# The seams between stages of a two-layer encoder: which squares the running sum takes, the fill products before a broadcast, and the order of products in the query, key, value stage

## The reference, cut to what matters

```python
for layer in range(2):
    h = h + 0.5 * rms_norm(swiglu(rms_norm(h, g[0]), w_in[layer, 0], w_out[layer, 0]), g[1])
    hn = rms_norm(h, g[2])
    m = attention_mixer(hn, ...) if layer % 2 == 0 else recurrent_mixer(hn, ...)
    h = h + rms_norm(m, g[3])
    h = h + 0.5 * rms_norm(swiglu(rms_norm(h, g[4]), w_in[layer, 1], w_out[layer, 1]), g[5])
return h[:, 16:]
```

## Time and profile before

| | |
|---|---|
| Median of 3 runs | 1137.19 us (1136.44, 1137.19, 1138.9) |
| Profiled execution, span from the first to the last instruction | 1134.5 us, 21273 instructions |
| PE / PEld / DVE / ACT / POOL busy | 96 / 92 / 63 / 49 / 10 % of the span |
| Mean granted TensorE clock | 0.991 of full |
| DMA | 169.65 MB, mean 150 GB/s |

### The profile page before, as it was taken

One profiled execution on the slowest core, in us unless ns is written; L12 is line 12 of the kernel. 1 busy time (PEld: TensorE's weight loads), 2 busy tenths in 40 slices (PEclk: granted clock), 3 DMA queues, 4 the chain that ended last, 5 costly groups with the idle time before them and its releaser, 6 DMA issues.

```text
span 1134.5 us, 21273 instructions
## 1 busy us (share of the span) xinstructions
PE 1094.0 (96%) x8622; PEld 1048.0 (92%) x8622; DVE 717.5 (63%) x1036; ACT 556.7 (49%) x830; POOL 114.5 (10%) x103
## 2 busy tenths in 40 slices
PE   6999999999999999999999999999997699999998
PEld 5999999998547999999999999999997699999997
DVE  5766655575554666665467666544889967666542
ACT  4544454453556554444445454444596556454541
POOL 3000000043000200000010000000377401000000
PEclk9999999999999999999999999999998899999999
DMA  8654445715002254635653644457153163645541
GB/s 250 212 190 148 162 149 184 247 61 174 1 1 73 77 186 158 203 111 182 198 187 127 201 155 148 150 184 243 55 186 111 38 223 112 211 160 176 170 137 38
DMA packets 166464, 169.65 MB, mean 150 GB/s; under 512 B 3312, under 2 KB 165416, under 8 KB 166392
## 3 DMA queue, kind: packets, MB, share of 16 engines
q1 hardware_dynamic: 166088, 168.16, 45.5%
q0 software_dynamic: 96, 0.28, 0.1%
q10 hardware_dynamic: 208, 0.20, 0.1%
HBM read 167.30 MB, written 1.05 MB: 148 GB/s over the span
## 4 chain that ended last, share of the span: by engine, by line
PE 88%; DVE 8%; ACT 1%; issue 1%; DMA 1%; POOL 0%; SPq 0%; DVEq 0%; ACTq 0%
PE bank L358 25%; PE bank L360 25%; PE bank L359 25%; PE bank L607 2%; PE bank L579 2%; DVE h L1120 1%; PE bank L593 1%; PE bank L386 1%; DVE mg L1116 1%; DVE xl L1083 1%; PE bank L366 1%; DVE gm L1368 1%; PE bank L479 1%; PE bank L377 1%; PE bank L374 1%
## 5 line engine op out<-in xcount | busy, mean ns | idle before, releaser
L1077 DVE TENSOR_TENSOR wl<-raw,wh 128x2048 fp32r<-128x2048 f32 (+2 forms) x178 | 366.3, 2078 | 173.8 <-ACT wh L717 173.4
L358 PE MATMUL bank<-xh,wl 128*128 128x272 f32 (+1 forms) x1552 | 448.5, 289 | 9.3 <-DVE xl L1373 7.8
L360 PE MATMUL bank<-xh,wh 128*128 128x272 f32 (+1 forms) x1552 | 446.6, 288 | 0.0
L359 PE MATMUL bank<-xl,wh 128*128 128x272 f32 (+1 forms) x1552 | 445.1, 287 | 0.0
L717 ACT ACTIVATE wh<-raw 128x2048 fp32r<-128x2048 f32 (+2 forms) x177 | 299.4, 1714 | 97.6 <-PE bank L360 97.6
L358 PEld LDWEIGHTS bank<-xh,wl 128*128 128x128 f32 x1552 | 293.5, 189 | 10.8 <-DVE xl L1373 8.0
L360 PEld LDWEIGHTS bank<-xh,wh 128*128 128x128 f32 x1552 | 293.4, 189 | 0.0
L359 PEld LDWEIGHTS bank<-xl,wh 128*128 128x128 f32 x1552 | 293.4, 189 | 0.0
L358 PE MATMUL bank<-ah,wl 128*128 128x272 f32 (+1 forms) x704 | 201.5, 286 | 0.0
L360 PE MATMUL bank<-ah,wh 128*128 128x272 f32 (+1 forms) x704 | 201.1, 286 | 0.0
L359 PE MATMUL bank<-al,wh 128*128 128x272 f32 (+1 forms) x704 | 201.0, 286 | 0.0
(11 more groups left out here) (157 smaller groups left out, 1181.2 us busy)
## 6 DMA issues: line engine op xcount, KB each, us to landing
raw<-in_ffn_w_in SPq DMA_DIRECT2D x88, 1024.0 KB, 5.3
raw<-in_ffn_w_out SPq DMA_DIRECT2D x32, 768.0 KB, 5.1
raw<-in_ffn_w_out SPq DMA_DIRECT2D x32, 640.0 KB, 4.2
raw<-in_rec_w_in SPq DMA_DIRECT2D x8, 1024.0 KB, 5.4
raw<-in_attn_w_qkv SPq DMA_DIRECT2D x6, 1024.0 KB, 5.0
raw<-in_attn_w_o SPq DMA_DIRECT2D x4, 1024.0 KB, 5.4
raw<-in_rec_gate_w SPq DMA_DIRECT2D x16, 256.0 KB, 3.7
raw<-in_rec_w_out SPq DMA_DIRECT2D x4, 1024.0 KB, 5.2
```

The lines of the kernel that those rows point to most:

```text
L358: pe.matmul(dst, b, mh, start=first, stop=False)
L359: pe.matmul(dst, a, ml, start=False, stop=False)
L360: return pe.matmul(dst, a, mh, start=False, stop=last)
L1077: dve.tensor_tensor(wl[:, slot(u), 0:kn * 256], w, wh[:, slot(u), 0:kn * 256].bitcast(F32), ALU.subtract).then_inc(w_ready, 1)
```

## The change

Four things change:

1. `ACC` is 9: DVE also adds tile 6's squares to `acc` in group 3, in the FFN behind the three weight splits of that group. `mean_of_projection` waits for `acc` and for `sqb[1]` only: 6 matmuls (12 records) instead of 9 (18).
2. The three fill products between the mean and the broadcast are gone. The six after it stay.
3. The query, key, value stage uses `chunk`, which takes the value products too: for each k first the 4 + 6 records with `xh[k]`, then the 2 + 3 with `xl[k]`.
4. `spread_r(1)` is gone, and `r_of_h` counts one less from there on.

```diff
-        ACC = 8
+        ACC = 9
...
-            def chunk(tiles, k, norm, t0):
+            def chunk(tiles, k, norm, t0, values=None, done=None):
...
+                if values is not None:
+                    x, wv_h, wv_l, parts = values
+                    for dst, a in parts:
+                        pe.matmul(dst, x[:, k, a:a + KT], wv_l, start=k == 0, stop=False)
+                        pe.matmul(dst, x[:, k, a:a + KT], wv_h, start=False, stop=False)
                 pe.wait_ge(x_ready, KC * norm + k + 1)
-                return [pe.matmul(dst, wh[...], xl[:, k, t0:L], ...) for dst, u, tile in tiles]
+                last = [pe.matmul(dst, wh[...], xl[:, k, t0:L], ...) for dst, u, tile in tiles]
+                if done is not None and k == KC - 1:
+                    for product_done in last:
+                        product_done.then_inc(done, 1)
+                return last
...
             def mean_of_projection(pj):
-                (three waits, three matmuls behind each: acc, sqb[:, 0], sqb[:, 1])
+                pe.wait_ge(acc_step, ACC * pj + ACC)
+                for c, a in enumerate(KTOK):
+                    pe.matmul(SUM_POST[0:KT, SC + c:SC + c + 1], acc[:, a:a + KT], mean_w, start=c == 0, stop=False, ...)
+                pe.wait_ge(sq_ready, 8 * pj + 8)
+                for c, a in enumerate(KTOK):
+                    last = pe.matmul(SUM_POST[0:KT, SC + c:SC + c + 1], sqb[:, 1, a:a + KT], mean_w, start=False, stop=True, ...)
                 last.then_inc(post_sum, 1)
-                keep_warm(3, bank[5])
                 pe.wait_ge(rt_ready, pj + 1)
...
             def attention():
                 for k in range(KC):
-                    pe.wait_ge(x_ready, KC + k + 1)
-                    (per k: 2 key products, then 3 value products, three matmuls each)
+                    values = [(bank[2 + c][0:KT, 0:NKV * HD], a) for c, a in enumerate(KTOK)]
+                    wv_h, wv_l = (v[:, slot(U_QKV + 1), k * 256:(k + 1) * 256] for v in (wh, wl))
+                    chunk([(bank[m][:, 0:L], U_QKV, 2 * k + m) for m in range(KT_N)], k, 1, 0, (xh, wv_h, wv_l, values), qk_done)
+                    for dst, a in values:
+                        last = pe.matmul(dst, xl[:, k, a:a + KT], wv_h, start=False, stop=k == KC - 1)
...
-                        if t == KT_N and k == 3:
-                            spread_r(1)
...
-                dve.wait_ge(r_spread, n + 1)
+                dve.wait_ge(r_spread, n + 1 if n == 0 else n)
...
                 def group(g, it=0):                 # DVE, FFN; the same in projection()
                     for j in range(3):
                         next_unit(g, j, it)
+                    add_squares(pj, 2 * g, it)
                     if g < 3:
-                        add_squares(pj, 2 * g, it)
                         add_squares(pj, 2 * g + 1, it)
```

More of the change, by code:

```diff
@@ L375, in chunk @@
                     pe.matmul(dst, a, xh[:, k, t0:L], start=False, stop=False)
+                if values is not None:
[3 more added lines that the diff above has]
+                        pe.matmul(dst, x[:, k, a:a + KT], wv_h, start=False, stop=False)
                 pe.wait_ge(x_ready, KC * norm + k + 1)
-                return [pe.matmul(dst, wh[:, slot(u), tile * P:(tile + 1) * P], xl[:, k, t0:L], start=False, stop=k == KC - 1)
+                last = [pe.matmul(dst, wh[:, slot(u), tile * P:(tile + 1) * P], xl[:, k, t0:L], start=False, stop=k == KC - 1)
                         for dst, u, tile in tiles]
+                if done is not None and k == KC - 1:
+                    for product_done in last:
+                        product_done.then_inc(done, 1)
+                return last
             def spread(dst, cols, heads=1):
@@ L472, in mean_of_projection @@
             def mean_of_projection(pj):
[L474 to L481, removed]
+                pe.wait_ge(acc_step, ACC * pj + ACC)
+                for c, a in enumerate(KTOK):
+                    pe.matmul(SUM_POST[0:KT, SC + c:SC + c + 1], acc[:, a:a + KT], mean_w, start=c == 0, stop=False, skip_group_check=True)
+                pe.wait_ge(sq_ready, 8 * pj + 8)
+                for c, a in enumerate(KTOK):
+                    last = pe.matmul(SUM_POST[0:KT, SC + c:SC + c + 1], sqb[:, 1, a:a + KT], mean_w, start=False, stop=True, skip_group_check=True)
                 last.then_inc(post_sum, 1)
-                keep_warm(3, bank[5])
                 pe.wait_ge(rt_ready, pj + 1)
@@ L1221, in projection @@
                 for g in range(4):
+                    add_squares(pj, 2 * g)
                     if g < 3:
-                        add_squares(pj, 2 * g)
                         add_squares(pj, 2 * g + 1)
```

## The result

The changed kernel took 1139.36 us (median of 11, 1138.34 to 1141.22), the kernel before 1136.73 us (11 runs, 1135.59 to 1138.9): ratio 1.0021, 95% interval 1.0013 to 1.003; the medians are 2.6 us apart. The profiled execution has a span of 1138.9 us (before 1134.5), 1140.67 us in all, so it is one of the longer ones, and a mean granted clock of 0.979 (before 0.991). Over its 11 executions the mean clock was 0.979 to 0.986, and the three of 0.979 are the three longest. The two spans are 4.4 us apart, and part of that is not the change's: the stretch from the last product of FFN 2 to that of the recurrent output took 136.91 before and 139.38 after, and between 136.43 and 138.50 in three other traces whose code there is that of the kernel before.

The account below looks back on a forecast made before the run. PE was taken to bound the kernel (88% of the chain of waits). Late seams 3 x 0.77, other seams -0.84 and query, key, value stage -0.75 gave +0.7 us on 1137.2, so 1137.9 us, range 1135.7 to 1140.8.

Parts of the forecast that it names:

- the likeliest case: Whole kernel: savings and late adds nearly cancel, 1137.9 us, chance 0.52.
- the first rival, the clock: Seams after FFN 0, 1 and 2: granted clock falls, 0.8 us each, 1140.3 us; chance 0.25.
- The sign of being wrong: Granted clock showing 0.5 behind an FFN seam, one of three signs named.
- The low end of the range, 1135.7: Bottom of the range 1135.7 to 1140.8, which includes a clock fall; the forecast's own bounds were 1135.5 to 1139.7.
- the third rival: FFN seams: the add isn't late, all six seams gain 0.28 us, 1133.8 us at most gain; chance 0.10.
- The late add: Seams after FFN 0, 1, 2: mean starts 1.31 us later, ends 0.82 later; +0.77 each without the fills.
- The other three seams: After attention output, recurrent output and last FFN: fewer mean records, broadcast 0.28 us earlier each, -0.84 us together.
- perhaps a fetch: Seam after FFN 0: DVE's first scale 0.39 us later than elsewhere; the delay may hide it, 0 to -0.39, taken as 0.
- The query, key, value stage: PE gains 0.67 us from order and 0.64 from the dropped broadcast; ACT passes on only 0.75 of 1.31.
- The sum without the clock: Whole kernel: late seams, other seams and query, key, value stage add to +0.7 us, 1137.9 us.
- the two halves: Whole kernel: savings and late adds, forecast to nearly cancel.
- Clock: Late seams: about 3.0 us of next to nothing on PE might lower the clock; earlier rows show no fall at a seam.

Follow-up runs that it names:

- early-add kernel: Changed kernel with the extra add of tile 6 written ahead of the third weight split in the FFN's last group: 1134.44 us, ratio 0.9977.
- late add with all waits filled: Changed kernel plus four fill products ahead of the mean after FFN 0, 1, 2 and two ahead of the broadcast in all six seams: 1136.28 us.
- fills in the wait: Changed kernel plus four fill products ahead of PE's wait for the sum after FFN 0, 1 and 2: 1136.92 us, ratio 1.0.
- late add alone: Kernel before with only the extra add behind the three weight splits and 12 mean records, three fills kept: 1140.87 us, ratio 1.0032.

## Why the prediction came out as it did

The time lay in the range; the move, +2.6 us where +0.7 was forecast, lies at the very edge of the 0.2% that I gave to no change, and the likeliest case was not what happened. It was the first rival, the clock, which I had at 1140.3 with a chance of 0.25. That the time is in the range says nothing for the forecast, since 1139.36 lies even within the bounds that I gave it without the rival (to 1139.7). The sign of being wrong that I had named, a clock of 0.5 behind an FFN seam, is what the trace shows. The low end of the range, 1135.7, doesn't follow from the sums either: a slower rival doesn't lift the 1135.5, and the third rival lay lower still.

- **The late add.** The mechanism and place were right. PE was to start the mean 1.31 us later; it was 1.15 (1.28 against 0.13). Most of the error is the time from DVE's end to PE's start: I took 0.16 from the first product of a stage, and it is 0.05 here (584.70 + 0.44 to 585.19). At the broadcast I had +0.77 and it was +0.57.
- **The other three seams.** -0.28 each was forecast; the broadcast came 0.45 earlier, by the same 0.05 instead of 0.16 at two waits. At the first scale it is 0.34 and 0.36 after the attention output and FFN 3, and nothing after the recurrent output, where DVE started at 3.26 as before: in the chain of the early-add kernel 0.40 us of "issue" stands there ahead of the scale. The same sort of 0.39 at the seam after FFN 0 I had named as perhaps a fetch and valued at 0; with the late add and a full clock it was gone (first scale 3.94 at all three late seams). The delay didn't hide it, since with the early add it was gone as well (2.91 after FFN 0, 2.92 after FFN 1). Why it stays at one place and goes at the other is open.
- **The query, key, value stage.** PE's 0.67 and 0.64 were right (0.69 and 0.68 in the traces). The 0.75 was not: I took the start of tile 2's squares for what PE waits for. The squares moved by 0.88, PE by 1.15, because the root that PE waits for stands behind a copy that waited for PE anyway. What was lost, 0.17, was lost earlier, at the wait for the gained copy of tile 0; that tiles 0 and 1 reach ACT 0.2 later I had, but not that PE waits there.
- **The sum without the clock.** Forecast +0.7; the terms as measured at full clock give 3 x 0.68 - 0.39 - 0.34 - 0.36 - 1.15 = -0.2, and the late add with all waits filled measured -0.3 (1136.28 against 1136.57, with an interval of 1 us to either side). That is 0.9 below the forecast, of which 0.4 is the query, key, value stage and 0.39 the first scale after FFN 0. That the two halves nearly cancel was right.
- **The step that failed: "Clock".** I put the fall at 1 in 4 because no row showed one at a seam. In the profiled execution it fell at all three late seams, and after the recurrent output and FFN 3 too. The one fall that I had read the earlier trace rows was no measure for a seam. The rule of the Trainium skill ("TensorE: Matmul & The Clock Gate", Part 1, "What's actually happening"), that the throttled clock is the default and activity releases it, had the better forecast. The traces bear it out as far as this: the clock went to 0.50 in late seams with 12 records of one column and no fills in them, and stayed at 1.00 with fills in every wait. Its worth: 1139.36 - 1136.73 = +2.6, less the -0.2 to -0.3 of the rest, is 2.8 to 2.9 us, and the stretches above give 1.05 and 1.17 for two of the three seams; I had 2.4 for the rival, 0.8 a seam.
- **A step that I didn't have.** The price of a fall depends on when in the seam it comes. Ahead of the broadcast it stretches the serial path: 0.91 us from broadcast to scale became 1.70. Behind it DVE's pace covers part: with fills in the wait the first scale was at 3.93 and 4.11 though the clock fell, and from FFN 1 to FFN 2 that kernel took 207.33, only 0.20 more than with all waits filled. And PE gave part of the delay back: in the kernel before it waited 0.61 us for the reciprocal of the next norm after FFN 1, in the changed one not at all; of the 2.73 us at the mean over h, 1.86 are left at the next seam.

## What to carry to other kernels

When a producer's last small step is put behind a long instruction of the same engine, its lateness is that instruction's end, not its own length: place it ahead (0.44 us of add behind a 2.29 us split cost +3.9 us together with the clock falls that it brought; ahead of it, with fills, the whole change gained 0.3 to 0.4%). Before taking out fill work, look at how long PE has neither products nor fills around it, and put fills inside the waits: one and two products inside them kept the clock and moved the first scale by 0.03 us, three behind a late wait did no good. Three on the path of the early-add kernel kept the clock as well, at a cost that these runs can't tell from nothing. At a few tenths of a percent, compare stretches between marks in the traces, since whole executions scatter by 2 to 3 us, while a stretch of the same code without a fall, the one behind FFN 2 apart, came out the same within 0.1 us in trace after trace. And a mark on an engine that moved less than its neighbours isn't yet the limit: look for what the other engine really waits for.

## What the runs showed of the hardware that I had not expected

Removing six fill records from a seam whose mean records ran on without a gap was enough for the granted clock to fall at five of six seams. There the longest idle time of PE before the fall was 0.46 us, and 18 one-column records stood in the seam. Busy time doesn't tell it either: the windows with falls have PE at 4.36 to 5.00 of 5 us, and one at 2.51 had none. In one trace the same code can keep the clock at one seam and lose it at the next (late add alone, after FFN 1 and FFN 2). A broadcast that PE had to wait for took 0.91 us for its six records at full clock, against 0.81 for one that came straight behind fills, so a tenth of a microsecond of the 0.45 gained was lost again at DVE.
